# Recurrence woven between the later projection blocks, its small products on four quarters of the array

## The reference, cut to what matters

```python
xn = rmsnorm(x, norm_mix_g)
p = xn @ w_in                              # (256, 8480)
gb, gc, xin = p_conv                       # 1024 columns each
conv = sum(conv_w[j] * shifted(gc * xin, 2 - j) for j in range(3)) * gb
# rwkv: r, k, v (1024 each) and 288 low-rank columns, each p + (p_prev - p) * mu
def step(state, inp):                      # 16 heads of 64, 256 steps
    sa = einsum('bhij,bhj->bhi', state, kk_t)
    state = (state * w_t + outer(-sa, kk_t * a_t) + outer(v_t, k_t))
    return state, einsum('bhij,bhj->bhi', state, r_t)
y = groupnorm(y) * ln_g + ln_b             # (y - mean) * rsqrt(var + eps) per head
rwkv = (y + bonus) * g                     # bonus = sum(r * k * r_k) * v per head
h = x + (sigmoid(gate_conv) * conv + sigmoid(gate_rwkv) * rwkv) @ w_out
out = rmsnorm(h + moe_ffn(rmsnorm(h, norm_ffn_g)), norm_final_g)
# moe_ffn: router, top 4 of 32, w1 (1024 x 2048), clamped SwiGLU, w2 (1024 x 1024) per expert
```

## Time and profile before

| what | us |
|---|---|
| median of three runs (lowest, highest) | 1351.99 (1351.64, 1354.59) |
| the profiled execution's own time | 1352.39 |
| its span in the trace | 1350.6 |
| PE busy in the span | 1256.0 (93%) |
| DVE busy | 327.5 (24%) |
| ACT busy | 215.2 (16%) |
| POOL busy | 61.4 (5%) |

### The profile page before, as it was taken

One profiled execution on the slowest core, in us unless ns is written; L12 is line 12 of the kernel. 1 busy time (PEld: TensorE's weight loads), 2 busy tenths in 40 slices (PEclk: granted clock), 3 DMA queues, 4 the chain that ended last, 5 costly groups with the idle time before them and its releaser, 6 DMA issues.

```text
span 1350.6 us, 22390 instructions
## 1 busy us (share of the span) xinstructions
PE 1256.0 (93%) x9961; PEld 667.8 (49%) x9961; DVE 327.5 (24%) x557; ACT 215.2 (16%) x341; POOL 61.4 (5%) x34
## 2 busy tenths in 40 slices
PE   6999999999999999999899899989989989989996
PEld 5888888899954333433333333333333333333332
DVE  1114484145534111211111111111211111211112
ACT  4121131143212100100001110000110000110001
POOL 0000000065311000000000000000000000000000
PEclk9999999999998999999999999999999999999999
DMA  9333353211196999999999999999999999999993
GB/s 304 130 125 125 129 183 125 78 57 26 32 413 255 430 428 436 428 432 431 427 430 434 433 428 432 427 431 430 434 431 433 428 428 429 437 427 432 432 429 143
DMA packets 43007, 449.74 MB, mean 333 GB/s; under 512 B 5264, under 2 KB 6544, under 8 KB 26480
## 3 DMA queue, kind: packets, MB, share of 16 engines
q1 hardware_dynamic: 39680, 445.58, 78.7%
q10 hardware_dynamic: 3280, 3.43, 0.9%
HBM read 447.95 MB, written 1.05 MB: 332 GB/s over the span
## 4 chain that ended last, share of the span: by engine, by line
PE 66%; DMA 30%; DVE 2%; ACT 1%; issue 1%; ACTq 0%; SPq 0%; DVEq 0%
DMA ring<-in_exp_w 30%; PE ps L701 20%; PE ps L407 17%; PE ps L736 10%; PE ps L474 5%; PE ps L667 3%; PE ps L658 2%; PE ps L590 2%; PE ps L476 1%; PE ps L490 1%; PE ps L714 1%; PE ps L691 1%; DVE work L1307 1%; PE ps L723 1%; PE ps L439 1%
## 5 line engine op out<-in xcount | busy, mean ns | idle before, releaser
L701 PE MATMUL ps<-ring,work 128*64 128x512 f32 x2048 | 471.4, 616 | 48.3 <-DMA ring<-in_exp_w 48.3
L701 PEld LDWEIGHTS ps<-ring,work 128*64 128x64 f32 x2048 | 150.9, 141 | 351.6 <-issue 276.2
L407 PE MATMUL ps<-work,ring 128*128 128x256 f32 (+1 forms) x1120 | 235.0, 380 | 0.6 <-ACT work L767 0.6
L736 PE MATMUL ps<-ring,work 128*64 128x512 f32 x1024 | 225.1, 592 | 0.0
L407 PEld LDWEIGHTS ps<-work,ring 128*128 128x128 f32 (+1 forms) x1120 | 201.6, 185 | 33.7 <-issue 5.0
L1296 DVE TENSOR_SCALAR work<-ps 128x512 f32<-128x512 f32 x32 | 22.1, 692 | 500.5 <-PE ps L701 500.5
L935 ACT ACTIVATE work<-work 128x512 f32<-128x512 f32 x32 | 20.1, 630 | 734.7 <-DVE work L1296 734.7
L736 PEld LDWEIGHTS ps<-ring,work 128*64 128x64 f32 x1024 | 72.4, 136 | 129.6 <-issue 129.6
L1312 DVE COPY work<-ps 128x512 f32<-128x512 f32 x32 | 22.1, 692 | 208.2 <-PE ps L736 208.2
L667 PE MATMUL ps<-work 64*128 64x512 f32 x264 | 65.6, 615 | 0.8 <-DVE work L1312 0.8
L658 PEld LDWEIGHTS ps<-sel,work 128*128 128x128 bf16 x1536 | 53.7, 118 | 24.3 <-issue 24.3
(11 more groups left out here) (228 smaller groups left out, 785.1 us busy)
## 6 DMA issues: line engine op xcount, KB each, us to landing
ring<-in_exp_w SPq DMA_DIRECT2D x64, 4096.0 KB, 29.2
ring<-in_exp_w SPq DMA_DIRECT2D x64, 2048.0 KB, 30.1
ring<-in_w_in SPq DMA_DIRECT2D x16, 2048.0 KB, 7.7
ring<-in_w_out SPq DMA_DIRECT2D x2, 2048.0 KB, 8.6
ring<-in_w_in SPq DMA_DIRECT2D x1, 1152.0 KB, 8.6
work<-in_x SPq DMA_DIRECT2D x2, 512.0 KB, 4.1
work<-in_x ACTq DMA_DIRECT2D x2, 512.0 KB, 4.1
out<-work SPq DMA_DIRECT2D x2, 512.0 KB, 2.7
```

What stands on the lines that cost most here:

```text
L407: last = mm(ps[b % 4][width * g:width * g + width, 0:T], chunk(n)[:, k, c0:c0 + width], XN[:, k, :], start=k == 0, stop=k == KT - 1)
L701: last = mm(ps[4 + part][64 * half:64 * half + 64, :], xe[:, k * CAP:(k + 1) * CAP], ring[:, slot(u, k), part * D + half * 512:part * D + ...
L736: last = mm(ps[7][64 * half:64 * half + 64, :], lhs, ring[:, slot(u, 8 + j), i * D + half * 512:i * D + half * 512 + 512], start=False, st ...
```

## The change

- w_in's order: low-rank, k, r, v, gate_rwkv, then for every two column blocks a chunk with half gc and half xin, and one with half gb and half gate_conv, each in two DMAs of 256 columns. From chunk 7 on only two buffers are used; ring 4 and 5 become matrices of the third and fourth token chunk.
- The low-rank products move up to blocks 3 to 10, 15 and 16 and the first head sums to block 12; from block 19 on the projection has only PSUM banks 0 and 1, and block b waits for whoever empties block b - 2. The operands are made while v is projected; DVE's reciprocal is cut in four.
- The 118 unit products of the recurrence (now with every transpose a product by an identity, and the mean of y taken away by a matrix `centre64` in the turn of V) are issued by `go`, which interleaves the instructions of one or two units. Some units stay on the two quarters of before; the others cross over: array rows 0 to 63 give output partitions 64 to 127, and rows 64 to 127 give 0 to 63 (an output, or the inputs, with `swap` 1). There are 53 calls of `go` with two units and 12 with one, in 32 groups between projection blocks; the last group, `turn_y(3)`, stands behind block 66. In each pair one unit is straight and the other crosses over, so that together they use all four quarters, and they write different PSUM banks.
- The state's addition is done by PE (`s_keep`), `centre` disappears from DVE.
- Gates and convolution are done block by block on 128x256 pieces by DVE and ACT, woven into their orders; the biases' splits on POOL come at the start. The last of them, `gate_in(7)`, `gate_conv(7)` and `add_conv(7)`, stand in DVE's order before `merge(0)` and `gate(1)`.
- `turn_y(2)` and `turn_y(3)` leave the output products. `turn_y(3)` waits for `y_gated` of 2, which `gate(1)` gives. The semaphore counts of the experts' loads are not changed.

```diff
-        stream = [(w_in, COL_LORA, LORA)]
-        for c0 in (COL_K, COL_R, COL_V, COL_GC, COL_XIN, COL_GB, COL_GATE_CONV, COL_GATE_RWKV):
-            stream += [(w_in, c0, CHUNK), (w_in, c0 + CHUNK, CHUNK)]
+        stream = [((COL_LORA, LORA),)]
+        for c0 in (COL_K, COL_R, COL_V, COL_GATE_RWKV):
+            stream += [((c0, CHUNK),), ((c0 + CHUNK, CHUNK),)]
+        for m in range(0, KT, 2):
+            for pair in ((COL_GC, COL_XIN), (COL_GB, COL_GATE_CONV)):
+                stream += [tuple((c0 + m * P, 2 * P) for c0 in pair)]
         NIN = len(stream)
-        stream += [(w_out, 0, CHUNK), (w_out, CHUNK, CHUNK)]
-        LOADS = [n % 3 for n in range(NIN)] + [0, 1]
+        LOADS = [0, 1, 2, 0, 1, 2, 0] + [1, 0] * 6
         def chunk(n):
...
+        def bank_of(b):
+            return ps[b % 4 if b < N_FIRST else b % 2]
+        def block_of(kind, m):
+            return kinds.index((kind, m))
+        def copies(kind, m):
+            return {"gate_rwkv": m, "gc": KT + 4 * (m // 2) + m % 2, "gate_conv": KT + 4 * (m // 2) + 2 + m % 2}[kind] + 1
...
-        NPE, ND, NA = 21, 15, 13
+        BANK_A, BANK_B = (2, 4, 6, 2), (3, 5, 7, 3)
+        Z, U, S_, Y_, TURN_Y = 4, 5, 6, 7, (2, 3, 2, 3)
...
+                elif b < N_FIRST:
                     pe.wait_ge(blk_shifted, b - 3)
                 else:
+                    kind, m = kinds[b - 2]
+                    if kind == "shifted":
+                        pe.wait_ge(blk_shifted, b - 1)
+                    elif kind == "xin":
+                        pe.wait_ge(x_mixed, m + 1)
+                    elif kind == "gb":
+                        pe.wait_ge(gb_mixed, m + 1)
+                    else:
+                        pe.wait_ge(blk_copied, copies(kind, m))
...
+            for b in range(N_FIRST):
+                project(b)
+                if 3 <= b < 11:
+                    decay_and_iclr(b - 3)
+                if b == 12:
+                    pe.wait_ge(lora_copied, 2 * KT)
                     pe.wait_ge(dve_step, 1)
                     head_sums(flat(i_TMP), (4, 5, 6, 7))
...
+            def go(*units):
                 for m in range(KT):
                     for q in range(2):
+                        for bank, a, b_, swap, opens, closes, done in units:
+                            o = ps[bank][rows(q ^ swap), cols(m)]
+                            if opens is None:
+                                last = mm(o, a(q, m), b_(q, m), start=True, stop=True)
+                            else:
+                                last = mm(o, a(q, m), b_(q, m), start=opens and m == 0, stop=closes, skip_group_check=True)
+                            if m == KT - 1 and q == 1:
+                                last.then_inc(done, 1)
...
+            def whole(bank, a, b_, swap, done):
+                return bank, a, b_, swap, None, None, done
...
...
+            def s_keep(c):
+                pe.wait_ge(s_opened, c + 1)
+                pe.wait_ge(s_taken, c)
+                return S_, const("ident64"), state(c), 0, False, False, s_kept
...
+            project(19)
+            project(20)
+            project(21)
+            project(22)
+            project(23)
+            project(24)
+            project(25)
+            bonus_sums()
+            go(upper(0))
+            go(lower(0))
+            project(26)
+            go(upper(1), f_rb(0))
+            go(lower(1))
+            project(27)
+            go(f_ak(0), upper(2))
+            go(lower(2))
+            go(f_rb(1), square(1))
+            go(f_rk(0), square(0))
+            project(28)
+            go(series(1, 0), turn_v(0))
+            go(f_ak(1), square(2))
+            project(29)
+            go(series(2, 0), turn_b(0))
+            go(series(1, 1), f_rk(1))
+            go(series(0, 0), f_rb(2))
+            project(30)
+            go(turn_k(0), series(2, 1))
+            go(f_ak(2), series(0, 1))
+            project(31)
+            go(f_rk(2), series(2, 2))
+            go(series(0, 2), turn_v(1))
+            project(32)
...
+            go(u_product(3), y_values(3))
+            project(55)
+            project(56)
+            project(57)
+            go(y_state(3))
+            go(turn_y(1))
+            go(y_u(3), turn_y(2))
+            project(58)
+            project(59)
+            project(60)
+            project(61)
+            project(62)
+            project(63)
+            project(64)
+            project(65)
+            project(66)
+            go(turn_y(3))
             pe.wait_ge(y_made, NCH)
             pe.sem_inc(w_used, 8)
...
             pe.wait_ge(merged, 2)
             out_product(0, 0, 0, 8).then_inc(wout_done, 1)
-            turn_y(2)
-            out_product(0, 1, 0)
-            turn_y(3)
-            out_product(0, 1, 4).then_inc(wout_done, 1)
+            out_product(0, 1, 0, 8).then_inc(wout_done, 1)
...
+            first_e(0)
+            first_e(1)
+            pool.wait_ge(dve_step, 7)
+            ptt(BON, BON, per_feature("ln_b"), ALU.add).then_inc(factors_ready, 1)
+            first_e(2)
+            pool.wait_ge(factors_ready, 1)
+            pool.wait_ge(scr_used, KT)
+            ptt(BON, BON, G, ALU.mult).then_inc(factors_ready, 1)
+            pool.wait_ge(factors_ready, 2)
+            ptt(G, G, per_feature("ln_g"), ALU.mult).then_inc(factors_ready, 1)
...
             link(nc.vector.memset(flat(i_BON), 1.0))
             link(nc.vector.memset(flat(i_BON).rearrange("p (c t) -> p c t", t=HEAD)[:, :, 0:1], 0.0))
+            for b in range(11):
+                shift(b)
+            v.wait_ge(blk_shifted, 11)
+            link(tt(KK, Kt, per_feature("k_k"), ALU.mult))
+            link(tt(TMP, KK, KK, ALU.mult))
+            v.sem_inc(dve_step, 1)
+            shift(11)
+            v.wait_ge(lora_copied, 2 * KT)
             link(nc.vector.tensor_tensor_scan(flat(i_CS), flat(i_BON), flat(i_SW), 0.0, ALU.mult, ALU.add))
+            shift(12)
...
+            shift(15)
+            link(tt(BON, AA, per_feature("k_a"), ALU.mult))
+            shift(16)
+            link(tt(BON, BON, inv[:, 27:35].unsqueeze(2).to_broadcast([P, KT, T]), ALU.add))
+            shift(17)
+            link(tt(Kt, Kt, BON, ALU.mult))
             v.wait_ge(act_step, 1)
-            link(nc.vector.reciprocal(flat(i_TMP), flat(i_TMP)))
+            for i in range(2):
+                nc.vector.reciprocal(flat(i_TMP)[:, 512 * i:512 * i + 512], flat(i_TMP)[:, 512 * i:512 * i + 512])
+            shift(18)
+            for i in range(2, 4):
+                last = nc.vector.reciprocal(flat(i_TMP)[:, 512 * i:512 * i + 512], flat(i_TMP)[:, 512 * i:512 * i + 512])
+            link(last)
             link(tt(KK, KK, TMP, ALU.mult))
+            v.wait_ge(blk_shifted, N_FIRST)
             v.sem_inc(dve_step, 1)
...
+                v.wait_ge(blk_done, b + 1)
+                tt(u_mix, u_mix, bank_of(b)[:, 0:T], ALU.mult).then_inc(x_mixed, 1)
+            def convolve(m):
+                v.wait_ge(x_mixed, m + 1)
+                link(ts(XI[:, m, :], u_mix, pc("conv2", m), None, ALU.mult))
+                link(stt(XI[:, m, 1:], u_mix[:, 0:T - 1], pc("conv1", m), XI[:, m, 1:], ALU.mult, ALU.add))
+                stt(XI[:, m, 2:], u_mix[:, 0:T - 2], pc("conv0", m), XI[:, m, 2:], ALU.mult, ALU.add).then_inc(conv_done, 1)
+            def gate_in(m):
...
+            link(tt(AA, AA, CS, ALU.mult))
+            v.sem_inc(dve_step, 1)
+            shift(19 + 3)
+            link(tt(BON, R, Kt, ALU.mult))
+            shift(19 + 4)
+            link(tt(BON, BON, per_feature("r_k"), ALU.mult))
+            v.sem_inc(dve_step, 1)
+            link(tt(Kt, Kt, CS, ALU.mult))
+            shift(19 + 5)
+            link(tt(R, R, TMP, ALU.mult))
+            v.sem_inc(dve_step, 1)
+            shift(19 + 6)
+            upper(0)
+            lower(0)
+            shift(19 + 7)
+            f_rb(0)
+            v.wait_ge(hs_copied, 4)
+            v.wait_ge(blk_shifted, N_SHIFT)
+            link(tt(BON, BON, V, ALU.mult))
...
+            convolve(7)
+            gate_in(6)
+            gate_conv(6)
+            add_conv(6)
+            gate_in(7)
+            gate_conv(7)
+            add_conv(7)
             merge(0)
+            gate(1)
             merge(1)
+            gate(2)
             merge(2)
+            gate(3)
             merge(3)
```

More of the change, by code:

```diff
@@ L229, in chunk_in @@
         def chunk_in(n):
-            return slot_in[2 * LOADS[n]], 16 * LOADS[0:n + 1].count(LOADS[n])
+            parts = [len(stream[i]) if i < NIN else 1 for i in range(n + 1) if LOADS[i] == LOADS[n]]
+            return slot_in[2 * LOADS[n]], 16 * sum(parts)
         def buffer_before(n):
@@ L321, in _ @@
             sp.dma_start(par[:], params).then_inc(const_in, 16)
-            for n, (w, c0, width) in enumerate(stream):
+            for n in range(NIN + 2):
                 if n >= 3:
@@ L479, in turn @@
-            def turn(bank, src):
-                for m in range(KT):
```

(113 more changed lines are left out.)

798 lines of the change are left out of this document (485 added, 313 removed).

## The result

| kernel | median, us (lowest, highest) | ratio to the kernel before, 95% interval |
|---|---|---|
| before, beside it | 1352.07 | 1 |
| changed | 1345.98 (1344.29, 1349.0; 5 runs) | 0.9948 [0.9934, 0.9963] |

Faster, as forecast, but by 6 us where 16 were forecast; 1345.98 lies in the range of 1323 to 1378 and at the edge of the forecast's own range (1325 to 1346). The profiled execution took 1349.0 (span 1347.2), the slowest of the five; the same kernel profiled once more in a later series took 1346.05 (span 1344.2).

What follows compares the result with a forecast made beforehand. PE's queue up to expert 0's start was taken as the bound, a gap-free weight transfer following. Terms -34.3 + 0.7 + 0.9 + 9.3 + 5 + 2.6 = -15.8 took 1352.39 to 1336.6, median 1336 us; range 1323 to 1378.

Steps and rivals of the forecast that it cites:

- A pair is one unit long: Recurrence: two units on four quarters take 0.93 us, as one does; the forecast, chance 0.55.
- B: Rival on the recurrence's pairs: loads of one row half queue up, a pair takes 1.87 us, total 1386; chance 0.15.
- C: Rival on the recurrence's pairs: 25 ns floor between matmul starts, a pair takes 1.68 us, total 1376; chance 0.08.
- E: Rival on the recurrence's pairs: they overlap only in part, 1.1 to 1.3 us each, total 1346 to 1356; chance 0.12.
- the first gap of the reciprocal: Before block 20: PE waits for shift 18 behind two quarters of DVE's reciprocal, 3.4 us lost.
- F: Rival at the experts: the weight transfer eats the gain if expert 0 starts before its weights land; no share given.
- The weave: Recurrence units between projection blocks: units and shape switches 73.3 us, plus 5 us for lateness.
- late masks: Inside the woven groups: seven of 32 groups late by one DVE operation of 0.69, 5 us; ends 0 and 22.
- the reciprocal in DVE's order: Before blocks 20 and 21: PE waits for shifts behind DVE's reciprocal, 3.4 and 5.9 us, together 9.3.
- two waits for ACT: In the projection: 0.7 us for the low-rank sigmoids and 0.9 us for the second `gate_lora`.
- from block 66 to expert 0: After the last projection block: the last gate's way through ACT and DVE idles PE 2.9 us, net 2.6 added.
- The second half of w_out: Issued after block 66: 8.6 us to landing, covered by 4 us of waits and a 7.1 us product; cost nothing.

Runs made afterwards that it cites:

- pairs_apart: The changed kernel with the two units of each pair issued one after the other; 1375.88 us, ratio 1.0165 to the kernel before.
- after_again: The changed kernel once more, unedited, as reference for a later series; 1346.28 us, ratio 0.9947 to the kernel before.
- filled: The changed kernel with unused constant products where PE idles, ahead of blocks 20 and 21 and behind block 66; 1343.36 us, ratio 0.9928.
- tail_short: The changed kernel with turn_y(3) ahead of block 63, gates earlier in DVE's order, and x's DMAs behind w_out, norm_ffn_g's DMA earlier; 1344.94 us, ratio 0.9939.
- router_late: The changed kernel with the three router DMAs behind x's copies on ACT's queue; 1346.14 us, ratio 0.9945 to the kernel before.
- ln_exp: The changed kernel with exp(-0.5 ln x) by ACT in place of the square root and DVE's reciprocal; 1334.37 us, ratio 0.9864.
- all_edits: The changed kernel with router DMAs later, Ln and Exp on ACT, the rearranged end, and low-rank and gate orders one block later; 1328.97 us, ratio 0.9832.

## Why the prediction was right in its mechanism and wrong in its size

**What held.** A pair is one unit long. In the chain above two singles, a pair and a single, and two pairs take the same 2.02, and the timeline inside a pair shows one start for each quarter about every 58 ns:

```profile
165.47 0.22 PE L537 MATMUL ps<-ring 64*64 64x64 f32 x1
165.48 0.22 PE L537 MATMUL ps<-cst,ring 64*64 64x64 f32 x1
165.49 0.22 PE L537 MATMUL ps<-ring 64*64 64x64 f32 x1
165.49 0.22 PE L537 MATMUL ps<-cst,ring 64*64 64x64 f32 x1
165.53 0.22 PE L537 MATMUL ps<-ring 64*64 64x64 f32 x1
```

Four starts between 165.47 and 165.49 and the next at 165.53. That rules out B (loads of the two column halves one after the other: pairs of 1.87), C (25 ns between starts: 1.68) and E (1.1 to 1.3). The blocks behind a group take 3.65, so the change back is 0.20, and the change into a group 0.16. The waits for the low-rank sigmoids (0.8) and the second `gate_lora` (0.9) came as forecast (0.7, 0.9), and so did the first gap of the reciprocal (3.34 for 3.4). The experts' transfer took none of it (F).

**The weave** took 78.4 us (144.56 to 364.52 less 41 blocks of 3.453), forecast 77.2. But the 5 us that I had given to late masks are none. PE is idle for 5.4 us in the whole stretch, and 5.3 of them are stops with nothing to wait for, 3.8 in the units and 1.5 in the blocks right behind them. The longest:

```profile
155.90 3.95 PE ps L537 x219
159.85 1.54 issue
161.39 0.34 PE ps L537 x5
```

In pairs_apart, whose instructions come at a slower pace (32 in 0.81 us for 64 in 0.93), the same row is 0.3. So the step failed in its cause and was right in its sum by luck. That PE's instructions don't arrive fast enough for the pairs is what these two kernels suggest, but a slower pace alone doesn't prevent the stops: the kernel before has them too, at 32 instructions in 0.93 us,

```profile
PE ps L474 <- issue: 1.9, 2, 1.3
```

the longer one of 1.34 us at 274.56, behind the first 252 instructions of the earlier trace rows. No run takes the supply of instructions apart, so the cause stays open.

**The steps that failed.** Expert 0 starts 11.7 us later than forecast (414.63 against 418.72 - 15.8 = 402.9):

| step, as the prediction put it | forecast | measured | missed |
|---|---|---|---|
| not in the sum: router's DMAs ahead of ACT's square root | 0 | 1.9 | 1.9 |
| not in the sum: the first three blocks slower, in this execution | 0 | 2.6 | 2.6 |
| the reciprocal in DVE's order | 9.3 | 11.9 | 2.6 |
| two waits for ACT | 1.6 | 1.7 | 0.1 |
| the weave (units, shapes, lateness) | 77.2 | 78.4 | 1.2 |
| from block 66 to expert 0 | 47.9 | 50.1 | 2.2 |

These are 10.6 of the 11.7; about half a microsecond more is in the two `gate_lora`, whose products take 1.97 and 1.99 instead of 1.73, and the rest I can't place. In after_again, whose first blocks are not slow, expert 0 starts at 412.42, and the miss is 9.5. Two terms of the prediction failed, and one was never in it.

*The reciprocal, 9.3.* DVE's order was priced rightly. The gaps were 7.6 instead of 9.3, but block 20 itself took 1.7 longer (5.41 for 3.72), and the second gap was shorter by just that (4.2, not 5.9). What the term left out is the work behind the second gap: blocks 21 to 25 took 2.6 us more, with a granted clock of 0.85. The gaps of PE were priced as gaps alone; filled gets 2.4 of the 2.6 back.

*The second half of w_out, "costed at nothing" at 8.6 us to landing.* It takes 13.3 us from the end of block 66, and this is what makes expert 0 start 50.1 us behind that block and not 47.9. The 8.6 came from a moment (267.10) when only the router's 0.15 MB went out beside it; now ACT's queue sends 1.5 MB (norm_ffn_g and x) from 364.61 on, and without them tail_short has 8.7 and no wait. The slower first output product (8.54 for 7.11) cost nothing here. In the five executions that have this end of the weave (the changed kernel twice, pairs_apart, router_late, ln_exp) the product took 8.1 to 8.5 in two, with a wait of 0.4 behind it, and 7.13 in three, with a wait of 2.0, and expert 0 starts 50.0 to 50.1 us behind block 66 in all five.

*The start, not in the sum.* The diff has it in plain sight: of three DMAs moved ahead on ACT's queue I followed only what they bring, not what they are put in front of, the square root. That is 1.9 us.

The 3.0 us between the profiled execution and the median are about the 2.6 of the slow first blocks; that the other four executions don't have these is not shown. By the spans the kernel gains 3.4 us, 6.0 with the 2.6 out, and 6.4 in after_again; the median says 6.

The Trainium skill ("TensorE: Matmul & The Clock Gate", Part 3), by which a weight load overlaps products in flight only where its row group differs, was set aside in the prediction because of w1's rows; the pairs bear that out, as far as the prediction's estimate of a load goes. In a pair each row half takes 32 loads beside products in flight on the same rows. At the 54 ns a load that the prediction estimates from the earlier trace rows they would need 1.73 us one after the other, and the pair takes 0.93, so by that estimate the loads of two column halves that share their rows ran beside each other. No run has a load of 64 columns by itself. This holds for 64x64 products on four quarters; no run here shows whole-array ones.

## What to carry to other kernels

Small products that each use a part of the array are best run beside each other, on disjoint quarters and different banks: 53 pairs gave 29 us over the same order with the units in turn, and without them the weave would have lost 22. When serial work is moved into an engine's busy stretch, go through every other engine's list and price the longest single instruction that now stands in front of a signal: one reciprocal that cost nothing before took 11 of the 28 us that the recurrence gave (107.6 before, 79.5 after, with `turn_y(3)`). Price an idle stretch of PE of 3 us or more above its length, for the work behind it may run at the lower clock, but only as far as no longer wait follows. Take a transfer's time to landing from a moment with the same traffic beside it, and follow each DMA issue in its queue to what stands behind it.

## What the runs showed of the hardware

- A quarter of the array starts one instruction of a float32 64x64 product about every 58 ns, and four quarters keep that pace together: 64 instructions in 0.94 us. Units on different quarters issued in turn still overlap at their edges, 0.81 us each for 0.93 alone.
- PE stops among such pairs with nothing to wait for, 6 times for 0.3 to 1.5 us in this kernel (5.3 us), hardly at all with the units in turn (0.3), but for 1.9 us in the kernel before. The cause is open.
- The clock after an idle stretch of 3.0 to 3.1 us at the end of the weave fell in four executions (0.76 over the 7 us behind it in all_edits and its repeat; the first output product took 8.5 and 8.1 instead of 7.1 in the changed kernel and its repeat) and not in four others (pairs_apart, router_late, ln_exp, tail_short: 1.00). After 3.3 and 4.2 us it fell in all five traces with these two gaps: block 20 took 5.41 us in each. At the start, two of the weave's ten executions that were profiled have the first three blocks 2.6 us longer; what decides it stays open.
- Ln and Exp on 128x2048 in ACT take 1.91 us each; the reciprocal of the same array takes DVE 12.95.
- 2 MB of w_out take 13.3 us from the end of block 66 to landing with 1.5 MB from ACT's queue beside them; with these moved away the two halves land after 8.7 (median; 10.5 before).
